# Decoder trunk with a mixture of experts: half a unit of weights kept on chip, the first gather in quarters, the final norm's gain ahead of the root

## The chip, the cores and the metric

One core of a Trainium2 chip runs the whole step as one program. The metric is the device time of that program in microseconds, the median of several runs. The host only lays the arrays out, and that is not timed.

## The reference, cut to what matters

264 tokens (256 of a prompt, 8 samples) of width 1024 pass through one layer, all in fp32:

```
x = x + mixer(rmsnorm(x, g_mix))                 # projections, spatial gating, short convolution
x = x + cross_attn(rmsnorm(x, g_xattn), mk, mv)  # 4 heads, 256 memory tokens; k, v from mem and w_k, w_v
x = x + moe(rmsnorm(x, g_moe))                   # 32 experts, top 4 by router logits
y = rmsnorm(x, g_final)                          # x * rsqrt(mean(x*x) + eps) * g_final

moe, for each expert e that a token chose:
    gate, up = split(xt @ w1[e] + b1[e])         # w1[e] is 1024 x 2048: 8 MB
    glu = min(gate, 7) * sigmoid(1.702 * min(gate, 7))
    out += g * (((clip(up, -7, 7) + 1) * glu) @ w2[e] + b2[e])   # w2[e] is 1024 x 1024: 4 MB
```

The outputs are y for prompt and samples, the keys and values of the memory, and three small states.

## The kernel before, in words

**Streams of weights.** SP's queue issues nearly all loads. In the front part (everything ahead of the experts) the weights come in chunks of 1 MB into a ring of 12 places, in the order of `FRONT_CHUNKS`; a chunk is issued when the matmuls that used its place have ended (`front_free`, L319). The experts' weights come in units of 2 MB: four of gate-up and two of down for each expert (`UNITS`). Eight unit buffers (L331) take turns; two of them lie in the arena, six in the ring. A unit's DMA is issued when TensorE has read the unit that lay there before (`unit_free`, L388). The first eight units go in while the attention and its output projection run (`first_units`, L376), the next eight in halves of 1 MB (L419 to L429), which wait for `half_used` and `w_used`; then `step` (L399) issues whole units, and the last down matrix comes in five parts (`LAST_PARTS`, L450).

**The start.** The raw memory tokens and the first chunk of w_k arrive in three parts, features 0 to 1, 2 to 3 and 4 to 7 of 8 (`FIRST_PARTS`). VectorE multiplies each feature tile by g_mem (L748), and TensorE forms key tiles 0 and 1 part by part (L1092 to L1100), then tiles 2 to 7 whole (L1101).

**Attention.** After the samples' scores (`sS`) TensorE turns the prompt's probabilities (`pT`, L1186). VectorE first finishes the samples' softmax (L863 to L867) and then copies the four turned heads (L870), and `attend` (L1188) reads them.

**Router and first gather.** TensorE turns the normalised tokens into rows (`to_tokens`, L1241), and ScalarE copies the six pieces and scales them (L626). That copy also exchanges columns, two by two, to fit the order of the gate-up rows in memory. VectorE picks the four experts, TensorE counts ranks (L1263 to L1271), and VectorE builds the one-hot matrix `p_hot` (L930) and the loop counts `iters` (L938, L939). TensorE gathers the tokens of the first two experts by matmuls with `p_hot` (L1281), four quarters of the features: two quarters before it reads the loop counts (L1290, L1291), and the other two during the first expert's gate-up products (L1329 to L1341).

**The expert loop.** `four_experts` (L1344) runs 8 times, four experts a time; 7 times in a loop and once at the end as `final`. In an iteration TensorE does the gate-up products of the next expert (L1307, four units), and between them turns this expert's gate-up result (`turn_gate_up`, L1311), gathers tokens (`gather_half`, L1368) and combines the expert before into the residual (L1298); then it does this expert's down products (L1425). VectorE adds bias and forms the gated product (`swiglu`, L967), ScalarE takes the sigmoid and copies (L638, L646). The order between the units is written by hand. In the last two iterations there is nothing more to gather, the turn of the last expert waits for ScalarE's copy (L1402), and the last down products run part by part (L1408 to L1416).

**The end.** Eight final products (L1439) are added to the residual (L1028). ScalarE squares (L693), TensorE sums, ScalarE takes the root (L695), VectorE the reciprocal (L736), TensorE spreads it over the partitions (L1450). VectorE then forms y with eight instructions, each with g_final and the spread root (L1034), and SP stores it in five DMAs (L461).

## Time and profile before

| what | us |
|---|---|
| median of 3 runs | 1196.09 (1193.36 to 1196.84) |
| the profiled execution, its own time | 1195.74 |
| its span | 1193.9 |
| TensorE (PE) busy | 1157.0 (97%) |
| VectorE (DVE) busy | 306.9 |
| ScalarE (ACT) busy | 157.7 |
| DMA, mean over the span | 384 GB/s, 458.34 MB |

The span is the time between the first and the last instruction of the trace; the execution's own time has 1.8 us more around it. Busy shares are means over stages with different limits: in the first 200 us TensorE works on dense projections while DMA is half idle, and in the expert loop both are busy nearly all the time. Which of them sets the pace there is to be read from who waits for whom. A number such as L1307 is a line of the kernel before; "idle before" is the time that an engine stood still ahead of an instruction, with what it waited for behind the arrow. Records of TensorE count each fp32 product as two instructions.

### The profile page before, as it was taken

How to read it: one execution, taken by the hardware profiler on the slowest of the kernel's cores; microseconds unless marked ns; L12 is line 12 of the kernel's file. 1: busy time of each engine (PE TensorE's matmuls, PEld its weight loads, DVE VectorE, ACT ScalarE, POOL GpSimd, SP SyncE). 2: the span in 40 equal slices, each digit the busy share in tenths (PEclk: the TensorE clock that was granted, in tenths of full speed). 3: DMA queues.
4: the chain of work that ended last, by engine and by line, in shares of the span. 5: the costliest groups of instructions: out<-in, count | busy, mean ns of one | idle time of the engine just before them, and what ended most of it. 6: DMA issues, size and time to landing. Idle time of an engine off the chain costs nothing.

```text
span 1193.9 us, 14908 instructions
## 1 busy us (share of the span) xinstructions
PE 1157.0 (97%) x5937; PEld 604.6 (51%) x5937; DVE 306.9 (26%) x638; ACT 157.7 (13%) x242; POOL 28.2 (2%) x63
## 2 busy tenths in 40 slices
PE   9999999999999999999999999999999999999997
PEld 8888888784434344444444343434343434343433
DVE  5124533332121212122222212121212121212124
ACT  2011011031101210121021011101110111010102
POOL 0000000000000000000000000000000000000000
PEclk9999999999999999999999999999999999999999
DMA  9963444998999999999999999999999999999995
GB/s 366 398 238 129 131 155 150 427 390 335 426 426 428 428 428 429 428 428 430 428 429 427 429 429 429 428 428 429 428 429 428 428 430 428 430 427 428 428 428 221
DMA packets 40398, 458.34 MB, mean 384 GB/s; under 512 B 6032, under 2 KB 6800, under 8 KB 8496
## 3 DMA queue, kind: packets, MB, share of 16 engines
q1 hardware_dynamic: 37440, 454.12, 90.7%
q10 hardware_dynamic: 2928, 3.80, 1.0%
q8 instruction: 21, 0.34, 0.1%
q14 instruction: 9, 0.07, 0.0%
HBM read 454.41 MB, written 3.23 MB: 383 GB/s over the span
## 4 chain that ended last, share of the span: by engine, by line
PE 72%; DMA 25%; DVE 1%; ACT 1%; issue 0%; SPq 0%; DVEq 0%; ACTq 0%
PE ps L1307 25%; PE ps L1084 15%; DMA ring<-in_w_dn 14%; PE ps L1425 13%; DMA arena<-in_w_dn 8%; PE ps L1281 7%; PE ps L1298 3%; DMA ring<-in_w_gu 3%; PE ps L1111 2%; PE ps L1318 2%; PE ps L1192 1%; DMA ring<-in_w_k 1%; PE ps L1177 1%; PE ps L1211 1%; PE ps L1167 1%; PE ps L1414 1%
## 5 line engine op out<-in xcount | busy, mean ns | idle before, releaser
L1307 PE MATMUL ps<-ring,arena 128*64 128x512 f32 x1536 | 349.9, 597 | 5.6 <-DMA ring<-in_w_gu 4.8
L1307 PEld LDWEIGHTS ps<-ring,arena 128*64 128x64 f32 x1536 | 103.1, 136 | 200.6 <-issue 184.7
L1084 PE MATMUL ps<-arena,ring 128*128 128x264 f32 (+1 forms) x800 | 178.9, 385 | 0.0
L1425 PE MATMUL ps<-ring,arena 128*64 128x512 f32 x736 | 165.4, 595 | 9.4 <-DMA ring<-in_w_dn 9.4
L1084 PEld LDWEIGHTS ps<-arena,ring 128*128 128x128 f32 x800 | 151.8, 190 | 25.3 <-issue 0.2
L1307 PE MATMUL ps<-arena 128*64 128x512 f32 x512 | 116.9, 598 | 2.8 <-DMA arena<-in_w_gu 2.4
L1020 DVE COPY arena<-ps 64x512 f32<-64x512 f32 x31 | 21.5, 694 | 369.1 <-PE ps L1425 369.1
L1425 PEld LDWEIGHTS ps<-ring,arena 128*64 128x64 f32 x736 | 52.7, 137 | 112.9 <-issue 106.8
L962 DVE TENSOR_TENSOR resid<-resid,ps 128x264 f32<-128x264 f32 x128 | 53.1, 429 | 173.3 <-PE ps L1298 172.8
L1281 PEld LDWEIGHTS ps<-arena 128*128 128x128 f32 x768 | 90.1, 195 | 14.8 <-issue 14.8
L1281 PE MATMUL ps<-arena 128*128 128x128 f32 x768 | 94.5, 280 | 1.8 <-ACT arena L626 1.8
L975 DVE TENSOR_TENSOR arena<-ps,par 128x512 f32<-128x512 f32 x64 | 44.0, 688 | 141.9 <-PE ps L1318 141.9
L638 ACT ACTIVATE arena<-ps 128x1024 f32<-128x1024 f32 x31 | 31.8, 1024 | 366.1 <-PE ps L1307 366.1
L1298 PE MATMUL ps<-arena 128*128 128x264 f32 x256 | 74.0, 412 | 0.6 <-DVE arena L1020 0.4
L1298 PEld LDWEIGHTS ps<-arena 128*128 128x128 f32 x256 | 43.4, 189 | 55.2 <-issue 50.0
L1307 PEld LDWEIGHTS ps<-arena 128*64 128x64 f32 x512 | 33.9, 136 | 64.9 <-issue 60.3
L1425 PE MATMUL ps<-arena 128*64 128x512 f32 x256 | 58.3, 597 | 5.0 <-DMA arena<-in_w_dn 5.0
L1318 PEld LDWEIGHTS ps<-ident,arena 128*128 128x128 f32 x256 | 33.4, 210 | 27.2 <-issue 27.2
L646 ACT ACTIVATE arena<-arena 128x512 f32<-128x512 f32 x32 | 20.2, 630 | 161.3 <-DVE arena L980 161.3
L1318 PE MATMUL ps<-ident,arena 128*128 128x128 f32 x256 | 39.5, 297 | 1.2 <-ACT arena L638 1.2
L682 ACT ACTIVATE arena<-ps 64x512 f32<-64x512 f32 x31 | 18.3, 590 | 143.4 <-PE ps L1425 143.4
L1425 PEld LDWEIGHTS ps<-arena 128*64 128x64 f32 x256 | 17.3, 137 | 39.1 <-issue 29.7
(201 smaller groups left out, 504.4 us busy)
## 6 DMA issues: line engine op xcount, KB each, us to landing
ring<-in_w_gu SPq DMA_DIRECT2D x92, 2048.0 KB, 32.6
ring<-in_w_dn SPq DMA_DIRECT2D x44, 2048.0 KB, 32.9
arena<-in_w_gu SPq DMA_DIRECT2D x32, 2048.0 KB, 33.7
arena<-in_w_dn SPq DMA_DIRECT2D x14, 2048.0 KB, 32.8
ring<-in_w_in SPq DMA_DIRECT2D x10, 1024.0 KB, 27.5
ring<-in_kc SPq DMA_DIRECT2D x8, 1024.0 KB, 4.8
ring<-in_vc SPq DMA_DIRECT2D x8, 1024.0 KB, 5.1
ring<-in_w_gu SPq DMA_DIRECT2D x8, 1024.0 KB, 8.8
```

Of the source, the lines that this page charges most:

```text
L638: nc.scalar.activation(gu_sb.rearrange("p (a b) -> p a b", a=2), ps[:, 0:2, :], ACT.Copy).then_inc(gu_copied, 1)
L646: nc.scalar.activation(sig[:], tb[:, :, 0:SLOTS], ACT.Sigmoid, scale=ALPHA).then_inc(sig_ready, 1)
L962: TTN(resid[:, m, :], resid[:, m, :], ps[:, 6 + m % 2, 0:T], ALU.add).then_inc(c_added, 1)
L975: TTN(both[:, :, h, :].rearrange("p (b m) s -> p b m s", b=2), turned[:, :, h, :].rearrange("p (b m) s -> p b m s", b=2), bc(bias, 3, [P, ...
L1020: copy(y_hot[row:row + 64, i // 2, 512:1024], ps[64:128, 4, :]).then_inc(y_right, 1)
L1084: last = mm(b[:, 0:width], w[:, k, P * (m % 2):P * (m % 2) + P], source(k), start=(k == 0), stop=(k == KT - 1))
L1111: last = mm(b[:, 0:256], mem[:, k, P * t:P * t + P], w[:, k, :], start=(k == 0), stop=(k == KT - 1))
L1281: last = mm(b[:, P * at:P * at + P], h_tok[t][:, first:first + P], p_hot[:, t, :], start=(t == 0), stop=(t == TT - 1))
L1298: mm(ps[:, 6 + m % 2, 0:T], y_hot[:, pair, P * m:P * m + P], g_hot[:, pair, :], start=True, stop=True).then_inc(c_filled, 1)
L1307: last = mm(ps[64 * h:64 * h + 64, bank + n, :], tile[:, k, SLOTS * half:SLOTS * half + SLOTS], w[:, at:at + 512], start=(k == 0), stop=(k ...
L1318: last = turn(ps[:, 2 + f // 4, P * (f % 4):P * (f % 4) + P], gu_sb[:, first:first + ROWS_DN * (P - 1) + 1:ROWS_DN], ident[:])
L1425: last = mm(ps[64 * h:64 * h + 64, 4, :], hid[i % 2][:, k, :], w[:, at:at + 512], start=(k == 0), stop=(k == KT - 1))
```

## The change

Seven edits:

1. The start: key tiles 0 to 3 are formed in two halves of the features. The second chunk of w_k comes in two halves, its first half ahead of the memory's second half, and `FIRST_PARTS` has two parts.
2. Half a unit of the last expert's gate-up weights (1 MB, the row of feature tile 7) is loaded in the front part into a place of its own at the end of the arena (`stash`), just ahead of the first key-cache chunk, and that half is no longer loaded in the expert loop. SP reads the loop counts before the other half. The arena grows from 22200 to 23280 elements, and `h_tok[2]`, `hid_odd` and `gu_sb` move.
3. Attention: the first two turned heads are copied before the samples' softmax is finished, under a semaphore of their own (`probs_copied`).
4. Router: TensorE writes the turned tokens to PSUM in the exchanged order, and ScalarE's copy of them is contiguous. The memset of `h_tok[2]` goes, since the gather reads only 8 rows of it. The first gather is one quarter before the loop counts are read, and one after each of the first three half units.
5. In iterations with odd i the gather comes after unit 0, the turn after unit 1, the combines after units 2 and 3; ScalarE copies the gathered tokens before its sigmoid.
6. The last expert's turn comes after the first two feature tiles of the down products of the expert before.
7. The end: g_final is multiplied in ahead of the root's arrival (tiles 0, 1, 2 and 5 on VectorE, 3, 4, 6 and 7 on ScalarE, into free ring places), and VectorE's last products cover two feature tiles each. y is stored in five DMAs, three on SP's queue and two on ScalarE's.

The diff, with lines of context, declarations of semaphores and the arena's size left out:

```
--- before.py
+++ after.py
@@ -57,7 +57,7 @@
-FIRST_PARTS = [(0, 2), (2, 4), (4, 8)]
+FIRST_PARTS = [(0, 2), (2, 4)]
@@ -76,9 +76,11 @@
+ARENA = 23280
-Y_PARTS = [(0, 2), (2, 4), (4, 6), (6, 7), (7, 8)]
+SCALED_EARLY = (0, 1, 2, 5)
+SCALED_LATE = (3, 4, 6, 7)
@@ -163,12 +165,9 @@
-        assert at <= 20700, at
-        h_last = view(at, D)
-        at += D
-        hid_odd = view(at, KT, SLOTS)
-        at += KT * SLOTS
-        assert at <= 22200, at
+        stash_at = ARENA - SLOT
+        assert at <= stash_at, at
+        stash = view(stash_at, SLOT)
@@ -187,7 +186,7 @@
-        h_tok = [view(at, D), view(at + D, D), h_last]
+        h_tok = [view(at, D), view(at + D, D), view(h_at + D, D)]
@@ -196,8 +195,9 @@
-        assert at + D <= h_at
-        gu_sb = view(h_at + D, D)
+        hid_odd = view(at + D, KT, SLOTS)
+        assert at + D + KT * SLOTS <= h_at
+        gu_sb = view(16 * T, D)
@@ -306,12 +307,19 @@
+        free_slot = NF % RING
+        scaled = ring[:, free_slot:free_slot + 2, :].rearrange("p a n -> p (a n)")[:, 0:KT * T].rearrange(
+            "p (k t) -> p k t", k=KT)
@@ -349,12 +357,20 @@
-                    landed[0] if part == 2 else part_landed[part], 16)
+                    part_landed[part], 16)
+            half = 256 * KT // 2
+            sp.dma_start(ring[:, 1, 0:half], w_k[1, :, 0:half]).then_inc(part_landed[2], 16)
+            sp.dma_start(mem_raw[:, KT // 2:, :], mem_t[:, KT // 2:, :]).then_inc(mem_in[2], 16)
+            for n in range(2):
+                sp.dma_start(ring[:, n, half:], w_k[n, :, half:]).then_inc(landed[n], 16)
-                if n == 0:
+                if n < 2:
+                if (kind, c) == ("kc", 0):
+                    rows = w_gu[NE - 1, KT - 2:KT].rearrange("k p n -> (k p) n")
+                    sp.dma_start(stash[:], rows.rearrange("(p j) n -> p (j n)", j=ROWS_GU)[:, SLOT:2 * SLOT]).then_inc(stash_in, 16)
@@ -396,9 +412,9 @@
-            def step(e, i, expert, next_expert):
-                for n in range(UNITS):
+            def step(e, i, expert, next_expert, units=range(UNITS)):
+                for n in units:
@@ -434,19 +450,27 @@
-                step(NE - 4 + i, i, NE - 4 + i, NE - 3 + i)
+                step(NE - 4 + i, i, NE - 4 + i, NE - 3 + i, range(UNITS if i < 2 else 3))
+                    step(again * NE - 2, 2, NE - 2, NE - 1, range(3, UNITS))
-                        step(again * NE + NE - 4 + i, i, NE - 4 + i, NE - 3 + i)
+                        step(again * NE + NE - 4 + i, i, NE - 4 + i, NE - 3 + i, range(UNITS if i < 2 else 3))
+            last_step = turns * 4 + 2
+            unit_free(last_step, 3)
+            n = (STEP_AT[2] + 3) % RING_UNITS
+            rows = w_gu[NE - 1, KT - 2:KT].rearrange("k p n -> (k p) n")
+            sp.dma_start(unit_buffer(n)[:, 0:SLOT],
+                         rows.rearrange("(p j) n -> p (j n)", j=ROWS_GU)[:, 0:SLOT]).then_inc(unit_landed[n], 16)
+            step(last_step, 2, NE - 2, NE - 1, range(4, UNITS))
@@ -456,10 +480,12 @@
-            for m, m_end in Y_PARTS:
-                sp.wait_ge(y_done, m_end)
-                sp.dma_start(y_t[:, m:m_end, :], resid[:, m:m_end, :]).then_inc(y_stored, 16)
-            sp.wait_ge(y_stored, 16 * len(Y_PARTS))
+            for m in (0, 4):
+                sp.wait_ge(y_done, m // 2 + 1)
+                sp.dma_start(y_t[:, m:m + 2, :], resid[:, m:m + 2, :]).then_inc(y_stored, 16)
+            sp.wait_ge(y_done, 4)
+            sp.dma_start(y_t[:, 6, :], resid[:, 6, :]).then_inc(y_stored, 16)
+            sp.wait_ge(y_stored, 16 * 5)
@@ -506,7 +532,6 @@
-            step(nc.gpsimd.memset(h_tok[2][:], 0.0), late_zero)
@@ -616,18 +641,16 @@
-            act.wait_ge(late_zero, 1)
+            act.wait_ge(mix_stored, 48)
-                act.wait_ge(grp, G[("htok", n)] + 1)
-                by_row = h_tok[n // 2][0:rows, 512 * (n % 2):512 * (n % 2) + 512].rearrange(
-                    "t (b j p) -> t b p j", b=2, j=ROWS_GU)
-                nc.scalar.activation(by_row, bank(("htok", n))[0:rows].rearrange("t (b p j) -> t b p j", b=2, j=ROWS_GU),
+                act.wait_ge(grp, G[("htok", n if n < 4 else 5)] + 1)
+                nc.scalar.activation(h_tok[n // 2][0:rows, 512 * (n % 2):512 * (n % 2) + 512], bank(("htok", n))[0:rows],
-            act.wait_ge(late_zero, 3)
+            act.wait_ge(late_zero, 2)
@@ -654,12 +677,12 @@
+                    if i % 2 and not final or i == 1:
+                        act.wait_ge(side_filled, pos + 2)
+                        copy_gathered(nxt, 1)
-                        if i % 2:
-                            act.wait_ge(side_filled, pos + 2)
-                            copy_gathered(nxt, 1)
@@ -694,6 +717,13 @@
+            for m in SCALED_LATE:
+                nc.scalar.activation(scaled[:, m, :], resid[:, m, :], ACT.Copy,
+                                     scale=par_of("g_final")[:, m:m + 1]).then_inc(late_scaled, 1)
+            act.wait_ge(y_done, 2)
+            act.dma_start(y_t[:, 2:4, :], resid[:, 2:4, :]).then_inc(y_stored, 16)
+            act.wait_ge(y_done, 4)
+            act.dma_start(y_t[:, 7, :], resid[:, 7, :]).then_inc(y_stored, 16)
@@ -862,12 +892,19 @@
+            dve.wait_ge(kv_stored, 32)
+            def copy_probs(h):
+                copy(probs_t[:, h, :, :], filled(("pT", h)).rearrange("p (m q) -> p m q", m=2)).then_inc(probs_copied, 1)
+            for h in range(2):
+                copy_probs(h)
-            TS(s_s[:], s_s[:], att_s[:, 8:9], None, ALU.mult).then_inc(emptied, 1)
-            dve.wait_ge(kv_stored, 32)
-            for h in range(HEADS):
-                copy(probs_t[:, h, :, :], filled(("pT", h)).rearrange("p (m q) -> p m q", m=2)).then_inc(emptied, 1)
+            TS(s_s[:], s_s[:], att_s[:, 8:9], None, ALU.mult).then_inc(emptied, 1 + HEADS)
+            for h in range(2, HEADS):
+                copy_probs(h)
@@ -940,9 +977,9 @@
-                ins.then_inc(ga_copied if n < 3 else emptied, 1 if n < 3 else 3)
-            dve.wait_ge(late_zero, 3)
+                ins.then_inc(ga_copied, 1)
+            dve.wait_ge(late_zero, 2)
@@ -951,9 +988,9 @@
-            copy(g_hot[0:NE, 1, :], filled("gT", T)[0:NE]).then_inc(emptied, 4)
+            copy(g_hot[0:NE, 1, :], filled("gT", T)[0:NE]).then_inc(emptied, 7)
@@ -1026,13 +1063,20 @@
-            inverse(5, rstd[:, 0, 0:T // 4])
+            for m in SCALED_EARLY:
+                if m == SCALED_EARLY[-1]:
+                    inverse(5, rstd[:, 0, 0:T // 4])
+                TS(scaled[:, m, :], resid[:, m, :], par_of("g_final")[:, m:m + 1], None, ALU.mult).then_inc(early_scaled, 1)
+            dve.wait_ge(early_scaled, len(SCALED_EARLY))
-            for m in range(KT):
-                tile = resid[:, m, :].rearrange("p (q t) -> p q t", q=4)
-                STT(tile, tile, par_of("g_final")[:, m:m + 1], ps[:, 1:5, 0:T // 4],
-                    ALU.mult, ALU.mult).then_inc(y_done, 1)
+            for m in range(0, KT, 2):
+                late = sum(n < m + 2 for n in SCALED_LATE)
+                if late:
+                    dve.wait_ge(late_scaled, late)
+                TTN(resid[:, m:m + 2, :].rearrange("p k (q t) -> p k q t", q=4),
+                    scaled[:, m:m + 2, :].rearrange("p k (q t) -> p k q t", q=4),
+                    bc(ps[:, 1:5, 0:T // 4], 1, [P, 2, 4, T // 4]), ALU.mult).then_inc(y_done, 1)
@@ -1053,6 +1097,8 @@
+                    elif before_it[0] == "pT":
+                        pe.wait_ge(probs_copied, before_it[1] + 1)
@@ -1088,21 +1134,32 @@
-            first_keys = ring[:, 0, :].rearrange("p (k n) -> p k n", k=KT)
+            first_keys = ring[:, 0:2, :].rearrange("p c (k n) -> p c k n", k=KT)
+            def keys(m, k_first, k_end):
+                for k in range(k_first, k_end):
+                    pe.wait_ge(mem_ready, k + 1)
+                    last = mm(bank(("k", m))[:, 0:NMEM], first_keys[:, m // 2, k, P * (m % 2):P * (m % 2) + P],
+                              mem[:, k, :], start=(k == 0), stop=(k == KT - 1))
+                return last
-                pe.wait_ge(landed[0] if part == 2 else part_landed[part], 16)
+                pe.wait_ge(part_landed[part], 16)
-                    for k in range(k_first, k_end):
-                        pe.wait_ge(mem_ready, k + 1)
-                        last = mm(bank(("k", m))[:, 0:NMEM], first_keys[:, k, P * m:P * m + P], mem[:, k, :],
-                                  start=(k == 0), stop=(k == KT - 1))
-                    if part == 2:
-                        last.then_inc(grp, 1)
-            for m in range(2, KT):
-                project("w_k", m, lambda k: mem[:, k, :], "k")
+                    keys(m, k_first, k_end)
+            pe.wait_ge(part_landed[2], 16)
+            for m in range(2, 4):
+                keys(m, 0, KT // 2)
+            for m in range(4):
+                if m % 2 == 0:
+                    pe.wait_ge(landed[m // 2], 16)
+                keys(m, KT // 2, KT).then_inc(grp, 1)
+            for m in range(4, KT):
+                project("w_k", m, lambda k: mem[:, k, :], "k")
@@ -1187,7 +1244,7 @@
-                pe.wait_ge(emptied, G[("pT", m // 2)] + 1)
+                pe.wait_ge(probs_copied, m // 2 + 1)
@@ -1243,7 +1300,9 @@
-                    last = turn(b[0:width, P * f:P * f + P],
+                    pair = b[0:width, 2 * P * (f // 2):2 * P * (f // 2) + 2 * P]
+                    by_row = pair.rearrange("t (j h i) -> t h i j", j=ROWS_GU, h=2)[:, f % 2]
+                    last = turn(by_row,
@@ -1278,14 +1337,17 @@
-                        last = mm(b[:, P * at:P * at + P], h_tok[t][:, first:first + P], p_hot[:, t, :],
+                        rows = P if t < 2 else NS
+                        last = mm(b[:, P * at:P * at + P], h_tok[t][0:rows, first:first + P], p_hot[0:rows, t, :],
-            pe.wait_ge(late_zero, 3)
+            pe.wait_ge(late_zero, 2)
-            gather(begin(("ga", 0)), 0, range(2), begun=True).then_inc(ga_filled, 1)
-            gather(begin(("ga", 1)), 0, range(2, 4)).then_inc(ga_filled, 1)
+            def gather_quarter(n):
+                return gather(begin(("ga", n)), n // 2, range(2 * (n % 2), 2 * (n % 2) + 2), begun=(n == 0))
+            gather_quarter(0).then_inc(ga_filled, 1)
@@ -1298,14 +1360,15 @@
-            def gate_up_unit(w, u, tile, half, bank=0):
+            def gate_up_unit(w, u, tile, half, bank=0, second=None):
+                    row = w[:, 0:SLOT] if k % 2 == 0 else w[:, SLOT:2 * SLOT] if second is None else second
-                            at = SLOT * (k % 2) + D * h + 512 * n
+                            at = D * h + 512 * n
-                                      w[:, at:at + 512], start=(k == 0), stop=(k == KT - 1))
+                                      row[:, at:at + 512], start=(k == 0), stop=(k == KT - 1))
@@ -1327,18 +1390,16 @@
-                if u < 3:
-                    pe.wait_ge(ga_copied, u + 1)
-                else:
-                    pe.wait_ge(emptied, NG)
+                pe.wait_ge(ga_copied, u + 1)
-                if u == 1:
+                if u < 3:
+                    gather_quarter(u + 1).then_inc(ga_filled, 1)
+                else:
-                if u in (1, 2):
-                    gather(begin(("ga", u + 1)), 1, range(2 * u - 2, 2 * u)).then_inc(ga_filled, 1)
+            pe.wait_ge(emptied, NG)
@@ -1384,14 +1445,23 @@
-                            first, last = gate_up_unit(unit(u), u, xg[((i + 1) // 2) % 2], (i + 1) % 2)
+                            kept = None
+                            if early and u == 3:
+                                pe.wait_ge(stash_in, 16)
+                                kept = stash
+                            first, last = gate_up_unit(unit(u), u, xg[((i + 1) // 2) % 2], (i + 1) % 2, second=kept)
-                            if u == 0:
+                            if i % 2:
+                                if u == 0:
+                                    gather_half()
+                                elif u == 1:
+                                    turn_gate_up(e)
+                                else:
+                                    combine_two(e, i, 2 * u - 4)
+                            elif u == 0:
-                                if i % 2:
-                                    gather_half()
@@ -1399,8 +1469,6 @@
-                    if early:
-                        turn_gate_up(e + 1)
@@ -1420,6 +1488,8 @@
+                            if early and k == 2:
+                                turn_gate_up(e + 1)
```

## Rows read from the trace of the kernel before

**Rows 1.** The page, part 2: what DMA moved in the 40 slices of the span.

```profile
GB/s 366 398 238 129 131 155 150 427 390 335 426 426 428 428 428 429 428 428 430 428 429 427 429 429 429 428 428 429 428 429 428 428 430 428 430 427 428 428 428 221
```

**Rows 2.** Waits of PE from 660 to 1060 us (total us, times, longest); PE's timeline.

```profile
PE ps L1425 <- DMA ring<-in_w_dn: 8.4, 10, 1.3
...
1139.99 3.65 PE L1425 MATMUL ps<-ring,arena 128*64 128x512 f32 x16 [0.59 <-DMA ring<-in_w_dn]
```

**Rows 3.** Timeline of the first 20 us (start, duration; idle before, releaser).

```profile
9.02 1.14 DVE L748 TENSOR_SCALAR arena<-arena,par 128x256 f32<-128x256 f32 x4 [2.19 <-DMA arena<-in_mem_t]
10.32 3.72 PE L1097 MATMUL ps<-arena,ring 128*128 128x256 f32 x16 [0.73 <-DMA ring<-in_w_k]
```

**Rows 4.** Timeline of the attention, 211 to 217 us.

```profile
212.80 2.48 DVE L870 COPY arena<-ps 128x512 f32<-128x512 f32 x4
213.63 3.69 PE L1192 MATMUL ps<-arena 128*128 128x256 f32 x16 [0.71 <-DVE arena L870]
```

**Rows 5.** Router, 259 to 270 us: one group with its mean ns, then timeline, then one instruction.

```profile
L626 ACT ACTIVATE arena<-ps,rstd_tok 128x512 f32<-128x512 f32 x4 | 3.9, 1151 | 0.3 <-DVE rstd_tok L736 0.3
...
259.88 2.38 PE L1246 MATMUL ps<-ident,arena 128*128 128x128 f32 x20
...
263.12 0.83 PE L1271 MATMUL ps<-arena,ones 128*128 128x32 f32 x6
263.60 0.70 DVE L930 TENSOR_TENSOR arena<-slot_no,rank 128x128 f32<-128x128 f32 x3
265.17 0.13 DVE L939 TENSOR_SCALAR iters<-arena 1x1 int32<-1x1 f32 x1
265.71 4.54 PE L1281 MATMUL ps<-arena 128*128 128x128 f32 x24 [1.76 <-ACT arena L626]
...
L1290 PEldq TENSOR_LOAD <-iters x1: 494/494/494, 267.0 to 267.0; - x1
...
L1291 PEldq SEQ_ASSERT  x1: 18/18/18, 268.6 to 268.6; - x1
```

**Rows 6.** Windows of 1 us: window, length, busy us by engine, PEclk, DMA share, GB/s.

```profile
267.00:268.00 1.00, 1.00 (x6) 1.00 (x6) 0.00 (x0) 0.20 (x1) 0.00 (x0) 0.50 0.11 45
...
1166.00:1167.00 1.00, 1.00 (x10) 0.88 (x11) 0.00 (x0) 0.00 (x0) 0.00 (x0) 1.00 1.03 434
```

**Rows 7.** A window of the stream's gap (columns of rows 6); two issues of SP's queue.

```profile
264.00:268.00 4.00, 2.29 (x11) 2.32 (x12) 1.17 (x8) 3.18 (x4) 0.00 (x0) 0.73 0.52 205
...
272.16 0.33 SPq L428 DMA_DIRECT2D arena<-in_w_dn  x1
...
326.75 0.33 SPq L366 DMA_DIRECT2D ring<-in_w_gu  x1
```

**Rows 8.** The end: timeline from 1160 us, a window (columns of rows 6), a group's mean.

```profile
1164.62 1.02 ACT L638 ACTIVATE arena<-ps 128x1024 f32<-128x1024 f32 x1 [12.11 <-PE ps L1307]
1165.78 1.23 PE L1318 MATMUL ps<-ident,arena 128*128 128x128 f32 x8 [1.20 <-ACT arena L638]
...
1170.23 0.69 DVE L988 TENSOR_TENSOR arena<-arena 128x512 f32<-128x512 f32 x1
1173.86 7.04 PE L1414 MATMUL ps<-ring,arena 128*64 128x512 f32 x32
...
1178.00:1179.00 1.00, 1.00 (x6) 0.29 (x4) 0.00 (x0) 0.00 (x0) 0.00 (x0) 1.00 0.11 45
...
1183.00 3.12 ACT L693 ACTIVATE arena<-resid 128x264 f32<-128x264 f32 x8
1186.91 0.57 DVE L736 RECIPROCAL rstd<-rstd 128x66 f32<-128x66 f32 x1 [1.25 <-ACT rstd L695]
1188.14 3.29 DVE L1034 SCALAR_TENSOR_TENSOR resid<-resid,par,ps 128x264 f32<-128x264 f32 x8 [0.66 <-PE ps L1450]
1189.05 2.93 SPq L461 DMA_DIRECT2D out_y_t<-resid  x5
...
L975 DVE TENSOR_TENSOR arena<-ps,par 128x512 f32<-128x512 f32 x64 | 44.0, 688 | 141.9 <-PE ps L1318 141.9
```

8 lines of the change are left out of this document (6 added, 2 removed).

## The prediction

> **What bounds the kernel now.** I read the bandwidth over the span first [rows 1]. Slices 4 to 7 (90 to 209 us) move 129 to 155 GB/s: DMA has room there. From slice 11 on it moves 426 to 430 GB/s and never more. The waits [rows 2] say which side sets the pace: between 660 and 1060 us TensorE waits for weights again and again, 8.4 us in 10 waits at one line alone. So in the expert loop the time is the stream's: what moves the stream's start moves everything behind it, and work saved on TensorE in between is not paid out. The last wait for weights comes at 1139.99 us [rows 2]. From there TensorE works through its own chain to the end, and DMA runs dry at about 1178 us (a share of 0.11 in that microsecond), ahead of TensorE's last down product at 1180.9 (1173.86 + 7.04) [rows 8]. Three stretches therefore count: the front part up to the router (TensorE's time), the gap in which the stream stands still at the router, and the tail behind 1140 us.
>
> **Start (edit 1).** TensorE waits 0.73 us for the third part of the first w_k chunk, until 10.32 us [rows 3]. In the change 16 records of tiles 2 and 3 stand there, worth 3.7 us by the 16 in the same row. Their weights are 512 KB behind the first 1 MB; the memory's second half lands behind them, by 512 KB at 428 GB/s some 1.2 us later than now, so VectorE's four products of 1.14 us [rows 3], now ended at 10.2, end near 11.4. TensorE gets to them at about 9.6 + 3.6 = 13.2 us. The second half of w_k's first chunk lands 1.2 us after 10.3, also ahead of 13.2. **Gain 0.7 us**; bounds 0 (the first half is late by as much) and 0.7. The sum of squares is formed 1.2 us later, but it is read by TensorE only after three tiles more.
>
> **Attention (edit 3).** TensorE stands 0.71 us, until VectorE has copied the first turned head [rows 4], which VectorE does only at 212.80, after the samples' softmax. The turns end at 212.9 (213.63 less 0.71), the first head's well before, so the first copy falls under the others. The other heads are copied 0.6 us each (2.48 for four) and are needed every 1.8 us (3.69 for two). **Gain 0.7 us**; bounds 0 and 0.7.
>
> **Stash (edit 2).** The 1 MB costs 2.45 us of DMA at 428 GB/s, in a stretch where two thirds of the rate lie idle [rows 1] and the ring is 12 chunks ahead: nothing. In the tail it takes 2.45 us from all that lands after it, but TensorE's own chain sets the end there, with DMA some 2.8 us ahead at the very end. **By itself 0**; bounds 0 and 2.4. What it buys is cover for edit 6. SP's reading of the counts, a few us earlier in its queue, stands in front of loads that wait some 30 us in the stream anyway; the same holds for the odd half's issue.
>
> **Router (edit 4), the largest term.** The stream: DMA's share falls to 0.52 in 264 to 268 us, that is, the eight units have landed at 266.1, and the next issue comes at 272.16, when the first half unit is used [rows 7]. Everything behind moves with that issue. Now: ScalarE's six copies take 1.15 us each, the last ends at 265.6, and TensorE waits 1.76 us for it; two quarters of the gather take 4.54 us, and the first products start at 270.25 [rows 5]. In the change the copies are contiguous. A contiguous copy of twice the elements takes 1.02 [rows 8], so I take 0.6 each: the turns end at 262.3, the last two copies at 263.5. TensorE is free at 263.95, VectorE's first one-hot tile is there at 263.85 [rows 5]; the quarter then runs from 264.05 to 265.45, at the speed of the turns' row. Then comes **a new wait**: the counts are written at 265.30 (L939), and TensorE's queue takes from 267.0 to 268.6 to read them, 1.62 us [rows 5]. Before, this lay under the gathering. Now it ends at 265.33 + 1.62 = 266.95, with VectorE's copy of the quarter (0.4 us) under it. First products at 267.05 instead of 270.2: **3.1 us earlier**, and so the issue.
>
> Then each half unit brings an issue. The second comes a quarter of the gather later (1.4 us) plus a half (1.8): 272.1 instead of 273.9, 1.7 earlier, and TensorE stays about 1.6 us ahead from there. Half units of 1 MB take 2.45 us in DMA, an issue with one quarter behind it 3.2, without one 1.8: over two issues 5.0 against 4.9, so the stream neither starves much nor catches up: the 3.1 us are kept, less a few tenths, which I leave to the range.
>
> Will it starve later? In the first experts the releases come unevenly; 326.75 us is the release behind unit 1 of the second expert [rows 7], when some 22 MB have been asked for since 272.16 and at 428 GB/s 21.4 have come: about 1.4 us in hand. With the stream 3.1 us earlier and TensorE only 1.6, 1.5 would be missing, but edit 5 puts the turn (1.2 us, [rows 8]) behind unit 1, so that the release comes 1.2 earlier still; units 2 and 3 likewise gain one combine each. 1.4 + 1.6 + 1.2 covers 3.1. **Edit 5 is worth 0** by itself, but keeps edit 4's gain; its turn is later by a gather and a unit, and the gated product, ready 4 us after the turn (1165.78 to 1170.92 less 1.2 for the turn, [rows 8]), has two units and two combines, over 9 us, before it is read.
>
> **The clock.** After the wait of 1.76 us TensorE ran at a granted clock of 0.50, that is 1.2 GHz (267 to 268 us) [rows 6], and the two quarters took 4.54 instead of 2.9. After the 1.2 us wait at 1164.6 it stayed at 1.00, 2.4 GHz [rows 6, 8]. The new wait of 1.6 us lies between, nearer to the one that cost. If the clock falls again, it falls on the first half unit, which the issue waits for: up to 1.7 us back. I take no fall, by little: the wait is shorter than the one that cost, and a whole quarter is gathered between the router's products and it. Both ends stay in the range: 3.1 and 1.4.
>
> **A rule against edit 4.** ScalarE's copy with exchanged columns took 1.15 us where a contiguous one takes 0.6 [rows 5, 8]; the change moves the exchange to TensorE's writes to PSUM, for which no row exists. The bounds for the 24 turns are 0 and ScalarE's surcharge per element (0.55/512 us, 0.14 us for a turn of 128): 3.3 us together, of which 2.8 before the ranks. I take 0, since a turn's pitch now (2.38/20 = 0.12 us for 128 columns) is slower than a column per cycle and leaves room. The Trainium skill, SBUF — State Buffer, section on Door 1, says that any non-contiguous PSUM pattern significantly slows matmuls, and gives no figure; by it the sum would lose up to those 2.8 us.
>
> **Tail (edits 6 and 7).** TensorE waits 1.20 us for the copy of the last gate-up result (1164.62 to 1165.64) [rows 8]; in the change the first four down products (1.8 us) stand there. Their weights landed about when unit 3 ended; the stash brings them 2.45 earlier. The gated product is ready 0.6 us later, at 1171.5, and is read at 1172.7. **Gain 1.2**; bounds 0.5 and 1.3. At the end VectorE's eight products take 3.29 us from 1188.14 [rows 8]; four over 528 elements, by the 512-element row from PSUM (0.69), take 2.7. The early products (three, about 1.1 us) lie between the last addition and the reciprocal at 1186.91, the fourth under TensorE's spread; ScalarE's four (0.39 each by 3.12 for eight) end at 1188.5, before VectorE's second pair. The stores: the last is now issued by two queues at once, as late after its product as before. **Gain 0.6**; bounds 0.2 and 0.9.
>
> **Sum.** 0.7 + 0.7 + 3.1 + 1.2 + 0.6 = 6.3 us. Against the profiled execution's 1195.74 that is 1189.4; the median stands 0.35 higher, so 1189.8. A measurement of this kernel can tell about 0.3% from no change, 3.6 us: faster means below 1192.5.
>
> **Rivals.**
> - *The clock falls in the new wait*, or the start gives nothing: 1.2 to 1.7 us less, 1191.3. For it, the 1.76 us case, against it the 1.2 us one. Chance 0.18.
> - *Scattered PSUM writes slow the turns*: 1192.6. For it the rule and ScalarE's row, against it the turns' slow pitch. Chance 0.15.
> - *The stream gives its head start back*: releases come too late near 327 us or in the first eight halves, and only 0.5 of the 3.1 is left: 1192.4, with the tail kept by DMA 1193.2. Chance 0.10.
> - *The end is DMA's after all*, the stash counts in full: 1187.3. Against it, no wait for weights behind 1140. Chance 0.05.
> - *Slower: the late turn in odd iterations.* If TensorE has to wait for the gated product ahead of each odd expert's down products, 16 waits come in. They are hidden while TensorE has slack against the stream, at least 8.4 us in 400 [rows 2], 1.2 us for two experts (24 MB, 58.8 us at 428 GB/s); beyond the slack each microsecond for two experts costs 15: 1 over gives 1204. The 9 us against 4 speak against it. Chance 0.05.
> - The forecast: 0.47.
>
> Faster by over 0.3%: the forecast, the first and the fourth rival and half of the second, 0.78. Within: 0.17. Slower: 0.05. Range 1187.0 to 1193.4.
>
> **What would show it.** The start: no wait for w_k at 10 us, attention's wait gone. ScalarE's copies at 0.6 us, turns still 2.4 us for 20, a new wait of 1.6 us before the first gate-up products, the first half issue 4.5 us earlier in the span (3.1 + 1.4). The stream at 428 GB/s from there. In the tail no wait before the last turn, four products of 0.7 us. Wrong it would be with turns over 0.2 us each, a clock of 0.50 behind the new wait, a DMA share under 0.95 between 315 and 335 us, or any wait of TensorE for the gated product.

## The result, and the profile after

The changed kernel takes 1211.26 us (median of 4 runs, 1210.37 to 1212.88), the kernel before 1195.73 in the same comparison: a ratio of 1.0134, 95% interval 1.0114 to 1.0154. The forecast was 1189.8, faster. It is 15.5 us slower.

The page of the changed kernel shows the answer in four places. First the busy times, the bandwidth in 40 slices, and the chain that ended last:

```profile
span 1208.7 us, 14918 instructions
PE 1198.2 (99%) x5937; PEld 618.9 (51%) x5937; DVE 307.3 (25%) x638; ACT 157.2 (13%) x246; POOL 27.2 (2%) x62
...
GB/s 363 406 221 175 141 139 181 428 369 366 407 415 427 428 430 427 429 428 429 429 427 429 428 428 430 427 428 429 427 431 427 428 429 427 430 428 427 428 381 37
...
PE 98%; DVE 1%; ACT 0%; issue 0%; DVEq 0%; POOL 0%; ACTq 0%; POOLq 0%
```

DMA still moves 428 GB/s in the middle, as in [rows 1], but it is finished earlier before the end: the last two slices show 381 and 37 GB/s, against 428 and 221, so DMA stops about one slice ahead of the end instead of half a slice (a slice is 30 us). In slices 11 and 12 it moves 407 and 415 GB/s, where the kernel before moved 426. TensorE is busy 99% of the span, and the chain lies on it for 98%. Of the waits for weights of [rows 2] none is left: between 300 and 1180 us TensorE waits for only these.

```profile
PE ps L1360 <- DVE arena L1057: 0.5, 1, 0.5
PE ps L1360 <- DVE resid L999: 0.2, 1, 0.2
```

The page's part 6 says the same from the other side: a unit of weights lands 15.8 us after its issue, where it was 32.6 before. Fewer loads stand in the queue, because more of the buffers hold weights that TensorE has not read yet.

```profile
ring<-in_w_gu SPq DMA_DIRECT2D x91, 2048.0 KB, 15.8
ring<-in_w_dn SPq DMA_DIRECT2D x44, 2048.0 KB, 15.7
```

So the bound has moved from the stream to TensorE. Which of its work grew, the chain of the changed kernel over one pair of experts shows (start, duration, what):

```profile
363.27 3.43 PE ps L1495 x16
366.70 4.22 PE ps L1341 x24
370.92 3.58 PE ps L1495 x16
374.51 3.43 PE ps L1370 x16
377.94 4.22 PE ps L1341 x24
382.16 3.58 PE ps L1370 x16
...
421.48 3.43 PE ps L1495 x16
```

The down products (L1495) and the gate-up products (L1370) take what they took, within 0.15 us. The gather (L1341) takes 4.22 us for 24 records, where the same 24 take 2.88 with all rows (below). Two experts take 421.48 - 363.27 = 58.2 us. In the chain of the kernel before the two matching down products stood at 361.11 and 416.27, that is 55.2 us. The groups by shape in 366 to 371.5 us show what is new in it (mean ns of a record, idle time before):

```profile
L1341 PE MATMUL ps<-arena 128*128 128x128 f32 x16 | 2.8, 300 | 0.0
L1341 PE MATMUL ps<-arena 8*128 8x128 f32 x8 | 1.9, 321 | 0.0
...
L1341 PEld LDWEIGHTS ps<-arena 128*128 128x128 f32 x16 | 2.1, 190 | 1.2 <-issue 0.8
L1341 PEld LDWEIGHTS ps<-arena 8*128 8x128 f32 x8 | 1.2, 182 | 0.5
```

A third of the records now has 8 rows (a record is one of the two instructions of a product, so the gather of 24 records has 12 products, every third with 8 rows). That is the part of the change which I had quoted and not costed: `rows = P if t < 2 else NS`.

The rest went much as forecast. The router and the end of the changed kernel, in time order:

```profile
261.27 0.66 ACT L649 ACTIVATE arena<-ps,rstd_tok 8x512 f32<-8x512 f32 x1
...
262.43 2.15 PE L1341 MATMUL ps<-arena 128*128 128x128 f32 x12
...
265.53 1.94 PE L1370 MATMUL ps<-arena 128*64 128x512 f32 x8 [0.95 <-DVE arena L979]
...
267.50 0.33 SPq L444 DMA_DIRECT2D arena<-in_w_dn  x1
...
1180.82 1.89 PE L1495 MATMUL ps<-ring,arena 128*64 128x512 f32 x8
1182.64 1.24 PE L1381 MATMUL ps<-ident,arena 128*128 128x128 f32 x8
1183.81 5.37 PE L1495 MATMUL ps<-ring,arena 128*64 128x512 f32 x24
1189.01 7.04 PE L1482 MATMUL ps<-ring,arena 128*64 128x512 f32 x32
...
1196.52 3.83 PE L1509 MATMUL ps<-arena 128*128 128x264 f32 x16 [0.48 <-ACT arena L702]
```

The first products begin at 265.53 (270.18 before) and the first issue comes at 267.50 (272.16 before, [rows 7]). In the tail the turn (L1381) stands between two down products, with no wait before it, where [rows 8] has 1.20 us.

### The profile page after: what moved, and what is told of

Its sections match the earlier page's. It is cut to its first block, busy times and chain, and to the rows that moved or that the text cites. A ratio compares the mean times of both kernels' runs of the same rounds, so it can differ in the third digit from the quotient of the medians.

```text
span 1208.7 us, 14918 instructions
## 1 busy us (share of the span) xinstructions
PE 1198.2 (99%) x5937; PEld 618.9 (51%) x5937; DVE 307.3 (25%) x638; ACT 157.2 (13%) x246; POOL 27.2 (2%) x62
## 4 chain that ended last, share of the span: by engine, by line
PE 98%; DVE 1%; ACT 0%; issue 0%; DVEq 0%; POOL 0%; ACTq 0%; POOLq 0%
PE ps L1370 37%; PE ps L1495 18%; PE ps L1130 14%; PE ps L1341 11%; PE ps L1360 6%; PE ps L1381 3%; PE ps L1168 2%; PE ps L1143 1%; PE ps L1423 1%; PE ps L1249 1%; PE ps L1268 1%; PE ps L1234 1%; PE ps L1224 1%; PE ps L1482 1%; PE ps L1092 0%; PE ps L1509 0%
## 5 line engine op out<-in xcount | busy, mean ns | idle before, releaser
L1370 PE MATMUL ps<-ring,arena 128*64 128x512 f32 x1528 | 348.5, 597 | 0.0
L1370 PEld LDWEIGHTS ps<-ring,arena 128*64 128x64 f32 x1528 | 102.5, 136 | 189.9 <-issue 185.9
L1130 PE MATMUL ps<-arena,ring 128*128 128x264 f32 (+1 forms) x768 | 171.7, 386 | 0.0
L1495 PE MATMUL ps<-ring,arena 128*64 128x512 f32 x736 | 164.4, 595 | 0.0
L1130 PEld LDWEIGHTS ps<-arena,ring 128*128 128x128 f32 x768 | 145.8, 190 | 24.6 <-issue 0.2
L1341 PE MATMUL ps<-arena 128*128 128x128 f32 (+1 forms) x768 | 137.4, 307 | 0.1
L1341 PEld LDWEIGHTS ps<-arena 128*128 128x128 f32 (+1 forms) x768 | 104.1, 187 | 53.7 <-issue 26.9
L1370 PE MATMUL ps<-arena 128*64 128x512 f32 x520 | 119.0, 598 | 1.0 <-DVE arena L979 1.0
L1495 PEld LDWEIGHTS ps<-ring,arena 128*64 128x64 f32 x736 | 50.8, 137 | 98.1 <-issue 97.1
L1360 PEld LDWEIGHTS ps<-arena 128*128 128x128 f32 x256 | 43.4, 189 | 55.3 <-issue 50.0
L661 ACT ACTIVATE arena<-ps 128x1024 f32<-128x1024 f32 x31 | 31.7, 1024 | 270.9 <-PE ps L1370 270.9
L1370 PEld LDWEIGHTS ps<-arena 128*64 128x64 f32 x520 | 34.5, 136 | 61.6 <-issue 58.4
L1495 PE MATMUL ps<-arena 128*64 128x512 f32 x256 | 58.1, 595 | 0.0
L1381 PEld LDWEIGHTS ps<-ident,arena 128*128 128x128 f32 x256 | 33.6, 211 | 26.0 <-issue 26.0
L664 ACT ACTIVATE arena<-ps 128x512 f32<-128x512 f32 x30 | 17.9, 597 | 205.1 <-PE ps L1341 205.1
L1381 PE MATMUL ps<-ident,arena 128*128 128x128 f32 x256 | 39.7, 298 | 0.0
## 6 DMA issues: line engine op xcount, KB each, us to landing
ring<-in_w_gu SPq DMA_DIRECT2D x91, 2048.0 KB, 15.8
```

The lines of the kernel that those rows point to most:

```text
L661: nc.scalar.activation(gu_sb.rearrange("p (a b) -> p a b", a=2), ps[:, 0:2, :], ACT.Copy).then_inc(gu_copied, 1)
L1130: last = mm(b[:, 0:width], w[:, k, P * (m % 2):P * (m % 2) + P], source(k), start=(k == 0), stop=(k == KT - 1))
L1341: last = mm(b[:, P * at:P * at + P], h_tok[t][0:rows, first:first + P], p_hot[0:rows, t, :], start=(t == 0), stop=(t == TT - 1))
L1360: mm(ps[:, 6 + m % 2, 0:T], y_hot[:, pair, P * m:P * m + P], g_hot[:, pair, :], start=True, stop=True).then_inc(c_filled, 1)
L1370: last = mm(ps[64 * h:64 * h + 64, bank + n, :], tile[:, k, SLOTS * half:SLOTS * half + SLOTS], row[:, at:at + 512], start=(k == 0), stop= ...
L1381: last = turn(ps[:, 2 + f // 4, P * (f % 4):P * (f % 4) + P], gu_sb[:, first:first + ROWS_DN * (P - 1) + 1:ROWS_DN], ident[:])
```

## The experiments

The theory (A): a change in the number of rows between neighbouring products costs TensorE some 0.17 us; a gather has eight such changes, the one at its edge counted; 32 gathers make TensorE the bound. Rivals: the tile's new place, the new order in odd iterations, or a price of the 8-row product itself.

**e1_full_rows.** All 128 rows again, all else as changed.

```
-                        rows = P if t < 2 else NS
+                        rows = P
```

> The changed kernel with one thing undone: the third product of each gathered tile reads all 128 rows of the sample tokens' tile again instead of 8 (the 120 other rows hold finite old values that meet zeros of the one-hot matrix). Theory A (the 8-row products cost about 0.17 us for each of their 8 records in a gather, and that alone makes the change slower): a gather of 24 records falls from 4.22 to about 2.9 us, two experts from 58.2 us of TensorE's time to about 55.2, waits for weights come back late in the loop, and the time is what the prediction had without this cost, about 1190 us (1188 to 1192). Rival B (the place is at fault: the tile now lies beside the gathered tokens): the gather stays at 4.22 us and the time at 1211. Rival C (the new order in odd iterations costs the 15 us): the gather gets shorter but the time stays above 1200.

Measured 1190.54 us (6 runs, 1189.92 to 1191.81) against 1195.39, ratio 0.9957 (0.9942 to 0.9971). A gather takes 2.88 us, two experts 55.5 (358.85 to 414.38), and TensorE waits for weights again:

```profile
358.85 3.43 PE ps L1495 x16
362.29 2.88 PE ps L1341 x24
...
414.38 3.43 PE ps L1495 x16
```

```profile
PE ps L1495 <- DMA ring<-in_w_dn: 5.9, 7, 1.3
PE ps L1495 <- DMA arena<-in_w_dn: 5.0, 4, 1.2
PE ps L1370 <- DMA ring<-in_w_gu: 3.4, 10, 0.7
PE ps L1370 <- DMA arena<-in_w_gu: 1.9, 3, 0.6
```

The place and the new order are as in the changed kernel, so rivals B and C fall. That one line costs 20.7 us; the other edits together give 4.9, and the difference, 15.8, is nearly the 15.5 of the result.

**e2_before_8rows.** The other way round: that line alone, in the kernel before.

```
-                        last = mm(b[:, P * at:P * at + P], h_tok[t][:, first:first + P], p_hot[:, t, :],
+                        rows = P if t < 2 else NS
+                        last = mm(b[:, P * at:P * at + P], h_tok[t][0:rows, first:first + P], p_hot[0:rows, t, :],
```

> The kernel before with only this part of the change: 8 rows in the third product of the gather, everything else as it was. Theory A: each gather takes 4.2 us, 1.34 more; some 31 gathers (30 in the loop and one in quarters) give 41 us more of TensorE's time, of which about 21.5 us (the sum of the waits for weights between 660 and 1140 us before) are swallowed by waits that vanish: 1195.7 + 20 = about 1215 us (1210 to 1220), and no wait for weights is left. Rival B (place): 1196 us. Rival C (order of odd iterations): 1196 us.

Measured 1214.05 us (2 runs), ratio 1.0159 (1.0139 to 1.018): 18.7 us slower, no wait for weights left. The gather takes 4.22 us here too, with the tile in its old place.

Not all of the 18.7 us is that line's. In the profiled execution TensorE's clock fell behind the old wait of 1.77 us and stayed low for longer than in the kernel before (columns as in [rows 6], the kernel before first):

```profile
268.00:272.00 4.00, 4.00 (x25) 2.74 (x25) 1.87 (x7) 0.00 (x0) 1.03 (x2) 0.84 0.01 4
...
268.00:272.00 4.00, 4.00 (x14) 3.10 (x15) 1.45 (x6) 0.00 (x0) 0.37 (x1) 0.50 0.02 5
```

It was 0.50 until about 279 us. The first gather in the loop begins at 316.54 us, where it began at 309.31: 7.2 us later, of which the 8-row products of the router's gathers explain 2.5 and the later start of the router 0.3. The other 4.5 or so are the clock's, by this estimate.

**e3_rows64 and e4_grouped.** Is it the size of the product, or the change of size?

```
e3:
-                        rows = P if t < 2 else NS
+                        rows = P if t < 2 else 64
e4:
+                for at, part in enumerate(parts):
+                    mm(b[:, P * at:P * at + P], h_tok[2][0:NS, first:first + P], p_hot[0:NS, 2, :], start=True, stop=True)
                 for at, part in enumerate(parts):
-                    for t in range(TT):
+                    for t in range(2):
```

> The changed kernel with 64 rows in the third product. If any change of the number of rows between neighbouring products costs, the gather stays near 4.2 us and the time near 1211 us. If only a product of very few rows costs, or the cost grows with the rows left out, the gather falls (with half the rows left out, half the surcharge: about 3.5 us) and the time to about 1196. If 64 rows cost nothing, about 1190 us.

> The changed kernel with the 8-row products of a gather put together at its beginning, so that the rows change between neighbouring products twice in a gather instead of eight times. This leaves the samples' share out of the gathered tokens (those products are overwritten); the number and size of the products stay. If the change between 128 and 8 rows costs (0.17 us each): a gather takes 2.9 + 0.3 = 3.2 us and the time falls to about 1191 us. If each 8-row product costs by itself (0.34 us): the gather stays at 4.2 us, the time at about 1211.

Each ran once. e4 leaves out the samples' share of the gathered tokens (the products with 128 rows write over it), so it is a test of time alone; its waits for the one-hot tiles move ahead of the gather.

With 64 rows the gather takes 4.23 us and the kernel 1210.24: half the rows cost as much as a sixteenth. With the 8-row products side by side the kernel takes 1192.14 us, and the gather falls into two pieces, 8 records and 16:

```profile
430.17 1.08 PE ps L1340 x8
431.25 1.98 PE ps L1345 x16
```

Together 3.06 us. An 8-row record takes 1.08/8 = 0.135 us beside others of 8 rows, a 128-row record 1.98/16 = 0.124. So an 8-row product is not dear; its neighbourhood to a 128-row product is.

The starts of the weight loads in the changed kernel show the place of the loss (single loads of one gather, those between left out):

```profile
366.96 0.19 PEld L1341 LDWEIGHTS ps<-arena 128*128 128x128 f32 x1
367.27 0.18 PEld L1341 LDWEIGHTS ps<-arena 8*128 8x128 f32 x1
367.38 0.18 PEld L1341 LDWEIGHTS ps<-arena 8*128 8x128 f32 x1
...
367.69 0.19 PEld L1341 LDWEIGHTS ps<-arena 128*128 128x128 f32 x1
```

Within one size a load follows the one before by 0.11 us, at 8 rows as at 128. Across a change, in either direction, it follows by 0.31: 0.20 more. In e4 that step stands once, at 430.87 to 431.18, and in e3 it is the same with 64 rows (436.06 to 436.38).

**e9_pairs and e11_pairs_again.** Fewer changes in a gather, all products kept: every second tile takes its three products in reverse order.

```
-                    for t in range(TT):
+                    order = range(TT) if at % 2 == 0 else range(TT - 1, -1, -1)
+                    for t in order:
...
-                                  start=(t == 0), stop=(t == TT - 1))
+                                  start=(t == order[0]), stop=(t == order[-1]))
```

> The changed kernel (8 rows) with the order of the three products turned round in every second tile of a gather, so that two 8-row products are neighbours: the rows change 4 times in a gather instead of 8, with the same products. If the cost is per change (0.17 us each): a gather takes 2.9 + 0.7 = 3.55 us and two experts 56.9 us, TensorE then has to wait for weights only near the end, and the time is 1191 to 1193. If it is per 8-row product: 4.2 us and 1211.

The gather takes 3.65 us. The expectations counted eight, four and two changes, with those at a gather's edges. Inside a gather there are seven in the changed kernel, four here and one in e4, and by this count a change costs (4.22 - 2.88)/7 = 0.19, (3.65 - 2.88)/4 = 0.19 and (3.06 - 2.88)/1 = 0.18 us. The cost follows the number of changes. The time, 1197.83 in a single execution, was above what I expected (1191 to 1193), and the windows of 263 to 272 us say why (window, length, busy, PEclk, DMA share, GB/s):

```profile
263.00:264.00 1.00, 0.56 (x4) 0.37 (x4) 0.33 (x1) 0.00 (x0) 0.00 (x0) 0.96 0.90 360
264.00:265.00 1.00, 0.30 (x2) 0.33 (x4) 0.86 (x6) 0.00 (x0) 0.00 (x0) 0.50 0.70 213
...
270.00:272.00 2.00, 2.00 (x10) 1.55 (x10) 0.13 (x1) 0.00 (x0) 0.00 (x0) 0.50 0.82 287
```

In this execution the clock fell to 1.2 GHz (0.50) in the new wait, as one rival of the prediction had it, and it was still there at 272: the first half unit took 3.68 us instead of 1.94. So the same kernel once more, with more executions.

> The kernel of e9_pairs once more, timed in rounds. In its one execution TensorE's granted clock was 0.50 from 263.9 to about 274 us, behind the wait for the loop counts, and the stream started late by that. Theory A (a gather with 4 changes of rows takes 3.65 us whatever the clock did at the router, and the late stream cost the rest): executions without the slow stretch give 1192 to 1194 us, against 1197.8 with it. Rival (the time of 1197.8 belongs to the order of the products): all executions lie at 1197 to 1198.

Median 1194.79 us (10 runs, 1193.17 to 1196.37), ratio 0.9993 (0.9984 to 1.0003). None of the ten reaches 1197, so the rival falls, but the median also lies above the 1192 to 1194 that I expected. Its profiled execution, too, had the clock low behind the wait, for a shorter stretch (0.58 on average in 264 to 268, 0.99 in the next 4 us), and a span of 1193.1. So both of my ends for the clock have been seen: it did not fall in the profile of the changed kernel, and it fell in these two and in e4's. The low level in this place costs a few microseconds where it lasts; how often it falls the runs do not say.

**e5_old_order.** From e1, edit 5 undone (TensorE's part is shown; ScalarE's copy of the gathered tokens goes back behind its sigmoid).

```
-                            if i % 2:
-                                if u == 0:
-                                    gather_half()
-                                elif u == 1:
-                                    turn_gate_up(e)
-                                else:
-                                    combine_two(e, i, 2 * u - 4)
-                            elif u == 0:
+                            if u == 0:
                                 turn_gate_up(e)
+                                if i % 2:
+                                    gather_half()
```

> e1_full_rows with the order of the odd iterations put back (turn and gather after unit 0, combines after units 1 and 2). e1's stream has lost 2.1 of its 4.7 us of head start, at least 1.7 of them before 292 us. Theory A (the new order keeps the releases near 315 to 335 us from coming late): DMA's share falls under 0.97 somewhere in 315 to 340 us, and the time rises by 0.5 to 1.5 us over e1, to 1191 to 1192. Rival (the stream is far enough behind after its early losses, so the order does nothing): DMA's share stays at 1.0 there, the last wait for weights stays near 1137.4 us and the time at 1190.5 us.

Measured 1190.77 us (4 runs), e1 1190.54. DMA's share in 312 to 340 us stays at 1.00 (418 GB/s against 427). The rival holds: in e1 edit 5 is worth nothing that can be measured in the time.

It does cost TensorE something. Two experts take 55.2 us in e5 (358.33 to 413.50) and 55.5 in e1, and the chain of e5 shows the two pieces that differ:

```profile
371.65 1.16 PE ps L1381 x8
372.82 2.68 PE ps L1341 x24
...
388.42 6.87 PE ps L1490 x32
```

The gather takes 2.68 us right behind the turns, whose products have its shape, and 2.88 behind the gate-up products, where edit 5 put it; the down products take 6.87 behind gate-up products and 7.02 behind a combine. In e1 the waits for weights hide these 0.35 us. In the changed kernel TensorE sets the pace from end to end, so there they cost about 5 us over some 15 pairs. That is an estimate; the changed kernel with the old order was not run.

**e6_no_stash and e7_old_turn.** From e1, the stash left out, or the turn put back.

```
e6:
-                            if early and u == 3:
-                                pe.wait_ge(stash_in, 16)
-                                kept = stash
e7:
-                            if early and k == 2:
-                                turn_gate_up(e + 1)
...
+                    if early:
+                        turn_gate_up(e + 1)
                     pe.wait_ge(hid_ready, e + 1)
```

In e6 the load of the stash goes too, and unit 3 of the last expert is loaded whole.

> e1_full_rows with the stashed half unit loaded in the stream again, as in the kernel before. Theory A (the tail is TensorE's chain, the stash only gives cover): the time stays within 1 us of e1 (1190.5 to 1191.5), because DMA had about 1 to 3 us in hand in the tail. Rival (the tail is DMA's, the stash counts in full): 2.45 us more, 1193 us, with waits for the last down parts.

> e1_full_rows with the last expert's turn back ahead of the down products of the expert before. Theory A: TensorE waits 1.2 us for the copy of the last gate-up result again, and the time rises by 1.2 us to 1191.7. Rival (something else would be late there): 1190.5.

e7: 1191.72 us (8 runs), 1.2 more than e1, with the wait of 1.2 us for ScalarE back. e6: 1191.37 (6 runs), 0.8 more. The single times of each overlap e1's, so for these two the traces weigh more than the medians. e6's tail shows where (TensorE, from 1160 us):

```profile
1160.40 1.94 PE L1489 MATMUL ps<-ring,arena 128*64 128x512 f32 x8 [0.25 <-DMA ring<-in_w_dn]
...
1172.68 3.65 PE L1476 MATMUL ps<-ring,arena 128*64 128x512 f32 x16 [0.39 <-DMA ring<-in_w_dn]
```

Without the stash TensorE waits for the down weights of both last experts. From the last common landmark (the second down unit of expert 29) to the end of the span it is 53.4 us in e6, 52.3 in e1, 53.5 in e7 and 53.9 in the kernel before. The stash is worth about 1 us as cover, not its 2.45 us of DMA time.

**e8_two_quarters.** The stream in e1 starts 4.66 us earlier than before, but its last wait for weights comes only 2.57 earlier (1137.42 against 1139.99). Windows show the loss early: from 268 to 292 us DMA moved 270, 309, 410, 320, 395 and 420 GB/s in windows of 4 us, together 8.50 MB, against 7.24 before; 1.25 MB more are 2.9 us at 428 GB/s, so 1.7 of the 4.66 were gone by then. One edit against that: two quarters of the gather ahead of the loop counts.

```
             gather_quarter(0).then_inc(ga_filled, 1)
+            gather_quarter(1).then_inc(ga_filled, 1)
             pe.wait_ge(iters_ready, 2)
...
-                if u < 3:
+                if u in (1, 2):
                     gather_quarter(u + 1).then_inc(ga_filled, 1)
-                else:
+                elif u == 3:
                     turn_gates()
```

> e1_full_rows with two quarters of the first gather ahead of the reading of the loop counts instead of one (so that the second quarter lies over the 1.37 us in which TensorE's queue reads them), and the other two after the first halves of units 1 and 2. Theory A (the stream's head start is lost because a quarter, 1.4 us, stands ahead of each of the early releases): the first issue stays near 267.5 us, the second comes about 1.4 us earlier (269.3 instead of 270.9), the stream keeps about 1.4 us more, the last wait for weights comes near 1136 us instead of 1137.4, and the time is about 1189.1. Rival (the stream loses its start elsewhere): 1190.5 us.

Measured 1188.41 us (4 runs, 1187.67 to 1188.89), ratio 0.9938 (0.9921 to 0.9955): 7.3 us faster than the kernel before and the best version of this study.

```profile
261.73 2.92 PE L1341 MATMUL ps<-arena 128*128 128x128 f32 x24
...
264.68 5.37 PE L1371 MATMUL ps<-arena 128*64 128x512 f32 x24
...
269.98 1.60 PE L1341 MATMUL ps<-arena 128*128 128x128 f32 x12
...
1134.48 3.65 PE L1496 MATMUL ps<-ring,arena 128*64 128x512 f32 x16 [0.49 <-DMA ring<-in_w_dn]
```

The second quarter fills the wait for the loop counts, and three half units follow without a quarter between them. The second issue comes at 268.36 instead of 270.91 us. The last wait for weights comes at 1134.48. Some 0.9 us of this stands in the span already ahead of the router in this execution, so of the 2.9 against e1 about 2.0 belong to the edit, as do 2.1 us of the median.

**e10_two_quarters_old_order.** e8 with edit 5 undone as in e5.

> e8_two_quarters with the order of the odd iterations put back. With e1 the order made no difference, and the stream there was late by its early losses. In e8 it is 2 us further ahead. Theory A (now the releases near 315 to 335 us come too late without the new order): DMA's share falls under 0.97 there and the time rises by 1 us or more over e8's, to 1189.4 or more. Rival (the order does nothing in either): within 0.5 us of 1188.4.

1189.26 us (4 runs, 1188.53 to 1189.77), 0.85 above e8. The windows of 328 to 332 and 332 to 336 us show 385 and 401 GB/s, where e8 has 418 and 434, but the share stays at 0.97 and more, and the last wait for weights is at 1134.55, the same as e8's. The medians lean to theory A and the landmark to the rival; a difference of this size is not settled by these runs.

## Why the prediction was wrong

- **The step that failed** is a term that the sum puts at nothing without a reason: the cut of the gather's third product to 8 rows, named ahead of the prediction. I treated fewer rows as free. It shows in the router's paragraph: "the quarter then runs from 264.05 to 265.45, at the speed of the turns' row". A quarter took 2.15 us in the changed kernel (12 records from 262.43) and not 1.4; in e1, with all rows, it took 1.58. At that place the surcharge cost nothing, since the wait for the loop counts covered it (0.95 us of wait instead of 1.37). It was paid in the gathers of the loop. e1 and e2 price the term: 20.7 us in the changed kernel, and up to 18.7 in the kernel before, some 4.5 of it the clock's by the estimate above. Its working would have been 1.34 us for each of 32 gathers, 43 us, of which the waits for weights can take only a part. With it "in the expert loop the time is the stream's" no longer holds: the changed kernel has no wait for weights at all.
- **The slack.** "At least 1.2 for two experts" was a bound from one row. The periods give it better: 58.7 us for two experts where the stream set the pace in the kernel before, 55.2 where TensorE did, so 3.5. The term added 2 x 1.34 = 2.7 to each pair, under that slack. It still cost time, because the slack was there only where the stream set the pace, from 660 to 1140 us: 8.2 pairs of 3.5 us, 29 us, while the term was paid in all 32 gathers, 43 us. The difference, 14 us, is about what e2 leaves of its 18.7 when the 4.5 of the clock are taken off. In the order of the changed kernel TensorE needs 55.5 us (e1), so the slack is 3.2, and it begins at about 720 us: 7.1 pairs, 23 us, and 43 less 23 is 20, against the 20.7 measured. All of these workings are estimates from the periods. The rival "slower" named the right resource, an overdrawn TensorE, with a wrong cause (the gated product read too early; no such wait shows), and so got a chance of 0.05; its bound for the slack could not have warned of a cost under it.
- **Start, attention.** Forecast 0.7 + 0.7; both waits are gone, and the output projection starts at 226.69 us instead of 228.29 (1.6 less). Right.
- **Router, first issue.** Forecast 4.5 us earlier in the span, measured 4.66, with the new wait for the loop counts nearly as worked out (1.37 us in e1): there TensorE's queue reads them from 263.9 to 265.3, and the first product follows at 265.53. Right. ScalarE's copies take 685 ns each instead of 1151. Right in kind.
- **"The 3.1 us are kept, less a few tenths."** Wrong even without the 8 rows. In e1 1.7 us were lost in the first eight halves. The working compared the rates of issue and transfer over two issues and found 5.0 us against 4.9; the windows of e1 show shares of 0.83 and 0.90 from 268 to 276 us and a rate of 320 GB/s in 280 to 284. I gave the rival "gives its head start back" 0.10; it was about half true. e8 shows what it cost: 2.1 us.
- **Edit 5 "keeps edit 4's gain", "worth 0 by itself".** The first is not shown: e5 equals e1, and e10 is 0.85 above e8. The second missed the 0.35 us of TensorE for each pair. The reserve of 1.4 us at 326.75 was also worked out too small: the trace's mean of 403 GB/s from 272.16 to 326.75 us gives 21.0 of the 22 MB asked for (in MB of 1024 x 1024 bytes), and not 21.4, so some 2.5 us were in hand.
- **The rule against edit 4.** The 20 turns with scattered writes take 2.38 us in the changed kernel, as they do in [rows 5]. Taking no cost was right. The Trainium skill, SBUF — State Buffer, section on Door 1, has non-contiguous PSUM patterns slow matmuls significantly; for these fp32 turns of 128 columns the trace does not agree.
- **Tail.** Forecast 1.2 for the turn; e7 gives 1.2. Forecast 0.6 for the end; from the first final product to the end of the span it is 12.53 us before and 12.18 after, 0.35. VectorE's last products took 2.55 us instead of 3.29 (by the row of 0.69 us they should have been put at 2.8, not 2.7), so 0.74 was saved there; but the span now ends 2.88 us behind the last of them instead of 2.47. "As late after its product as before" did not hold for the stores. The stash: forecast 0 by itself with 0 to 2.4 as bounds; 0.8 by the medians of e1 and e6.
- **The sum without the missing term.** e1 is the kernel that the sum describes: 1190.54 against 1189.8, and a gain of 4.9 us over the kernel before in the same comparison against 6.3. The stream's lost head start is what is short, less what the stash gave.

## What to carry to other kernels

Cost every line of a diff that changes the shape of an instruction in a loop, above all one that looks like less work, and multiply by its count. A product with fewer rows between products with 128 rows was no saving here but a surcharge; if such products must be, put them side by side (e9 in pairs; e4, of which only the time counts), or pad them with rows that meet zeros (e1). Slack between a stream and an engine is to be read from the two periods and from when the buffers run out, not from the waits at one line. And a wait for a register's value is a place to put work that needs no register (e8).

## What the runs showed that I had not expected

- Changing the number of rows of neighbouring fp32 products, 128 to 8 or 128 to 64 and back, costs TensorE 0.18 to 0.19 us for a change (2.88, 3.06, 3.65 and 4.22 us for 0, 1, 4 and 7 changes in 24 records). The number of rows itself made no difference between 8 and 64 (4.22 and 4.23 us). The Trainium skill, TensorE: Matmul & The Clock Gate, section Step-by-step: what each phase is for, says that the time of a weight load goes by its columns and not by its rows, and that loads are pulled ahead of running products where the row groups don't conflict or the load goes to the background buffer. Within one size the traces agree (a load of 8 rows takes 182 ns, one of 128 rows 190 ns, and either follows the one before by 0.11 us). Across a change of size the next load starts 0.20 us later than that, together with its own product and not ahead of it (367.27 and 367.69 us). Why it can't go ahead there no run here shows.
- The granted clock fell to 0.50 around the wait ahead of the first gate-up products in three profiled executions with the new wait (e9: a wait of 1.14 us, low from 263.9 us to about 274; e11: 0.98 us, shorter; e4: waits of 0.49 and 0.58 us, low from about 263.9 to 267), and stayed at 1.00 in eight others (the changed kernel, e1, e3, e5, e6, e7, e8, e10), among them e5 with a wait of 1.54 us. So the length of the wait does not order the cases. With the old wait of 1.76 us it fell in both profiles, of the kernel before and of e2. The three falls with the new wait are of the two kernels that change the order inside the gather; whether that is the cause was not tried.
